# Whole half units of three weight units at the seams of a six-sublayer step, and tiles normalised in another order

## What is computed

```python
def modulate_in(x, g_pre, mod, j):
    return rmsnorm(x, g_pre) * (1.0 + mod[:, :, 3 * j + 1]) + mod[:, :, 3 * j]

def gated_residual(x, out, g_post, mod, j, weight):
    return x + weight * mod[:, :, 3 * j + 2] * rmsnorm(out, g_post)

def shortconv_mixer(h, w_in, conv_w, conv_b, w_out):
    gb, gc, xin = jnp.split(h @ w_in, 3, axis=-1)
    return (gb * dwconv_centred(gc * xin, conv_w, conv_b)) @ w_out

def swiglu(h, w13, w2):
    a, g = jnp.split(h @ w13, 2, axis=-1)
    return (jax.nn.silu(g) * a) @ w2
```

## Time and profile before

| | us |
|---|---|
| median of 3 runs | 2453.85 (2453.64 to 2454.42) |
| profiled execution | 2452.03 |
| its span | 2450.2 |
| PE busy | 2404.4 (98%), granted clock 0.998 |
| DVE busy | 1757.9 (72%) |
| ACT busy | 981.3 (40%) |
| POOL busy | 436.1 (18%) |

### The profile page before, as it was taken

One profiled execution on the slowest core, in us unless ns is written; L12 is line 12 of the kernel. 1 busy time (PEld: TensorE's weight loads), 2 busy tenths in 40 slices (PEclk: granted clock), 3 DMA queues, 4 the chain that ended last, 5 costly groups with the idle time before them and its releaser, 6 DMA issues. The chain is left out here.

```text
span 2450.2 us, 38986 instructions
## 1 busy us (share of the span) xinstructions
PE 2404.4 (98%) x15173; PEld 2204.5 (90%) x15173; DVE 1757.9 (72%) x2469; ACT 981.3 (40%) x1917; POOL 436.1 (18%) x462
## 2 busy tenths in 40 slices
PE   6999999999999999999999999999999999999998
PEld 6998999889889789979988997998899989989997
DVE  5988785675554679778846878885577759856863
ACT  4442343533445455324434442443511154423432
POOL 1220120201115222102213210220200022201211
PEclk9999999999999999999999999999999999999999
DMA  7526333385212453353252426334154433243333
GB/s 228 164 61 217 94 86 128 115 261 154 54 51 74 108 181 87 125 160 87 78 172 104 131 71 229 87 87 138 52 180 139 135 107 90 71 148 98 87 111 113
DMA packets 347229, 297.96 MB, mean 122 GB/s; under 512 B 38799, under 2 KB 296839, under 8 KB 347047
## 3 DMA queue, kind: packets, MB, share of 16 engines
q1 hardware_dynamic: 341798, 278.64, 37.7%
q0 software_dynamic: 5248, 16.83, 1.8%
HBM read 280.57 MB, written 14.80 MB: 121 GB/s over the span
## 5 line engine op out<-in xcount | busy, mean ns | idle before, releaser
L2013 DVE TENSOR_TENSOR w_lo<-w_raw,w_hi 128x512 fp32r<-128x512 f32 (+1 forms) x249 | 211.4, 852 | 243.6 <-ACT w_hi L1419 242.6
L1419 ACT ACTIVATE w_hi<-w_raw 128x512 fp32r<-128x512 f32 (+1 forms) x249 | 188.3, 760 | 467.1 <-DMA w_raw<-in_ffn_w_dram 201.5
L913 PE MATMUL psum<-w_hi,act_hi 128*128 128x512 f32 x800 | 318.3, 398 | 0.4 <-DVE w_lo L2013 0.4
L915 PE MATMUL psum<-w_hi,act_lo 128*128 128x512 f32 x800 | 317.2, 396 | 0.0
L914 PE MATMUL psum<-w_lo,act_hi 128*128 128x512 f32 x800 | 317.0, 396 | 0.0
L1046 PE MATMUL psum<-hT_hi,w_hi 128*128 128x320 f32 x912 | 281.9, 309 | 0.5 <-DVE z_quarters L2301 0.5
L1048 PE MATMUL psum<-hT_hi,w_lo 128*128 128x320 f32 x912 | 281.8, 309 | 0.0
L1047 PE MATMUL psum<-hT_lo,w_hi 128*128 128x320 f32 x912 | 281.8, 309 | 0.0
L1046 PE MATMUL psum<-t_hi,w_hi_more 128*128 128x320 f32 x608 | 187.9, 309 | 0.0
L1048 PE MATMUL psum<-t_hi,w_lo_more 128*128 128x320 f32 x608 | 187.9, 309 | 0.0
L1047 PE MATMUL psum<-t_lo,w_hi_more 128*128 128x320 f32 x608 | 187.8, 309 | 0.0
(11 more groups left out here) (303 smaller groups left out, 5926.4 us busy)
## 6 DMA issues: line engine op xcount, KB each, us to landing
w_raw<-in_ffn_w_dram SPq DMA_DIRECT2D x96, 512.0 KB, 5.1
w_raw_next<-in_ffn_w_dram SPq DMA_DIRECT2D x80, 512.0 KB, 5.2
w_raw<-in_ffn_w_dram SPq DMA_DIRECT2D x148, 256.0 KB, 3.2
ada_tile_ffn<-in_ada_w_dram SPq DMA_DIRECT2D x56, 512.0 KB, 3.9
ada_direct<-in_ada_w_dram POOLq DMA_DIRECT2D x32, 512.0 KB, 5.7
w_raw<-in_ab_w_in_dram SPq DMA_DIRECT2D x28, 512.0 KB, 4.1
w_raw<-in_sc_w_in_dram SPq DMA_DIRECT2D x24, 512.0 KB, 4.7
ada_tile_sc<-in_ada_w_dram SPq DMA_DIRECT2D x24, 512.0 KB, 3.6
```

What stands on the lines that cost most here:

```text
L913: mm(out, a_hi, b_hi, start=first, stop=False)
L915: return mm(out, a_lo, b_hi, start=False, stop=final)
L1419: A(dst, src, ACT.Copy).then_inc(w_hi_ok, 1)
L2013: V.tensor_tensor(d_, a, b.bitcast(F32), ALU.subtract).then_inc(w_lo_ok, 1)
```

## The change

1. The first three units of sublayers 1 to 5 run as whole half units: units 0, 1 and 2 on the first 320 tokens, then the same on the last 320. Unit 2 gets two PSUM banks of its own. Unit 0, the *lead*, gets raw, high and low buffers of its own; it is loaded during the sublayer before (`load_lead`, behind the loads of the gate and the modulation columns) and split in its out phase.
2. In the seams of sublayers 2 and 5 tile three is turned behind unit 0, and the order of DVE and ACT is written anew: a tile is normalised ahead of the wait for the next tile's evacuation. In all seams the slices between which tiles 0 to 2 are turned are others.
3. `STEPS` of "ab" and "sc" are later by a unit or two; `LOADS` stays. In "sc" the split of unit 3 is moved ahead of the convolution.

The core of the diff:

```diff
-STEPS = {"ffn": [2 + j for j in range(16)], "ab": [1, 1, 2, 2, 3, 3, 4, 4, 5, 6, 7, 9, 10, 10, 11, 11], "sc": [2] + [2 + j for j in range(23)]}
+STEPS = {"ffn": [2 + j for j in range(16)], "ab": [2, 2, 3, 3, 4, 4, 5, 5, 6, 7, 8, 9, 10, 10, 11, 11],
+         "sc": [4, 4, 5, 6, 7, 7, 8, 9, 10, 10] + [11 + j for j in range(14)]}
...
+        lead_at = lambda s: arena + 20 * TOK * 4 + HELD[KD] * 4096 if SUBS[s - 1] == "ab" else j0
+        lead_raw = {s: at(f"w_raw_lead{s}", [P, KD, P], lead_at(s)) for s in range(1, len(SUBS))}
+        lead_hi = {s: at(f"w_hi_lead{s}", [P, KD, P], lead_at(s) + 4096, F32R) for s in range(1, len(SUBS))}
+        lead_lo = {s: at(f"w_lo_lead{s}", [P, KD, P], lead_at(s) + 8192, F32R) for s in range(1, len(SUBS))}
...
+            def load_lead(s):
+                l, f = s // 3, s % 3 // 2
+                w, col = {"ffn": (ffn_w13[l, f], FF), "ab": (ab_w_in[0], COL["qa"]), "sc": (sc_w_in[0], D)}[SUBS[s]]
+                dma(lead_raw[s][:], w.rearrange("(p k) n -> p k n", k=KD)[:, :, col:col + P]).then_inc(lead_loaded, 16)
...
-                        for u in range(SC_IN):
+                        for u in range(1, SC_IN):
                             n = nb + u
                             sp.wait_ge(w_lo_ok, n - 1)
...
                         load_gate(s)
                         load_cols(s + 1)
+                        load_lead(s + 1)
...
-            def unit_part(p, h, c0, c1, ready):
+            def unit_part(s, r, h, ready):
+                n = plan[s][0]["nin"] + r
+                out = (THIRD if r == 2 else IN[n % 2])[:, h, 0:HT]
                 for k in range(KD):
                     if k % (KD // 2) == 0:
                         pe.wait_ge(hT_ready, ready[k // (KD // 2)])
-                    hi, lo = w_hi[:, p, k, :], w_lo[:, p, k, :]
+                    hi, lo = (lead_hi[s][:, k, :], lead_lo[s][:, k, :]) if r == 0 else (w_hi[:, n % 2, k, :], w_lo[:, n % 2, k, :])
                     for a, b in ((hi, hT_hi), (hi, hT_lo), (lo, hT_hi)):
-                        last = mm(IN[p][:, h, c0 - h * HT:c1 - h * HT], a, b[:, k, c0:c1],
+                        last = mm(out, a, b[:, k, h * HT:(h + 1) * HT],
                                   start=(k == 0 and a is hi and b is hT_hi), stop=(k == KD - 1 and a is lo))
                 return last
 
...
-                h0, h3, h4 = [HM(s, 2)] * 2, [HM(s, 3)] * 2, [HM(s, NT - 1), HM(s, NT)]
-                for r, h, c0, c1, ready in ((0, 0, 0, HT, h0), (1, 0, 0, HT, h0),
-                                            (0, 1, HT, 4 * P, h3), (0, 1, 4 * P, TOK, h4), (1, 1, HT, TOK, h4)):
-                    n = ph["nin"] + r
-                    if s and r == 0 and c0 == HT:
-                        turn_x(s, NT - 1)
-                    pe.wait_ge(w_lo_ok, n + 1)
-                    need(pe, in_evac[n % 2], inv(ph, n) - 1)
-                    last = unit_part(n % 2, h, c0, c1, ready)
-                    if c1 == TOK:
-                        last.then_inc(pe_unit, 1)
+                for h in range(2):
+                    for r in range(3):
+                        n = ph["nin"] + r
+                        if h == 0 and r == 1 and not early(s):
+                            turn_x(s, 3)
+                        if h == 0 and r == 2:
+                            turn_x(s, NT - 1)
+                            pe.wait_ge(hmod_ok, HM(s, 3))
+                        pe.wait_ge(*((w_lo_ok, n + 1) if r else (lead_lo_ok, LEAD_LO(s))))
+                        if r < 2:
+                            need(pe, in_evac[n % 2], inv(ph, n) - 1)
+                        last = unit_part(s, r, h, [HM(s, NT - 1), HM(s, NT)] if h else [HM(s, 2)] * 2)
+                        if h:
+                            last.then_inc(pe_unit, 1)
...
+                    if s > 1:
+                        pe.wait_ge(in_evac[UB[s] % 2], inv(plan[s][0], UB[s]) + 1)
...
+                SEAM_TURN = {True: {2: 4, 3: 2, 4: 0}, False: {2: 4, 3: 2, 4: 2}}
                 for t in range(NT):
-                    order = list(range(K)) if t < NT - 1 else ring[0::2] + ring[1::2] + list(range(held))
+                    order = list(range(K)) if t < NT - 1 else ring[1::2] + ring[0::2] + list(range(held))
...
-                        if t >= 2 and s + 1 < len(SUBS) and z == (4 if not early(s + 1) else 3 if t == 2 else 0):
+                        if t >= 2 and s + 1 < len(SUBS) and z == SEAM_TURN[early(s + 1)][t]:
...
+            def split_lead(s):
+                act.wait_ge(lead_loaded, 16 * s)
+                A(lead_hi[s][:], lead_raw[s][:], ACT.Copy).then_inc(lead_hi_ok, 1)
...
+                    if final and u == K and s + 1 < len(SUBS):
+                        split_lead(s + 1)
...
+                finish_tile(s - 1, 0)
+                add_out(s - 1, 0)
+                finish_tile(s - 1, 1)
+                norm_x(s, 0)
+                add_out(s - 1, 1)
+                norm_x(s, 1)
+                finish_tile(s - 1, 2)
+                add_out(s - 1, 2)
+                split_h(s, 0)
+                norm_x(s, 2)
+                finish_tile(s - 1, 3)
+                split_h(s, 1)
+                add_out(s - 1, 3)
+                split_h(s, 2)
+                norm_x(s, 3)
+                finish_tile(s - 1, 4)
+                split(n + 1)
+                add_out(s - 1, 4)
+                split(n + 2)
+                norm_x(s, 4)
+                split_h(s, 3)
+                split_h(s, 4)
 
...
-                        split(n + 2, i, 6)
+                        if not (first(i) and jj == 0):
+                            split(n + 2, i, 6)
...
+                        if first(i) and jj == 0:
+                            split(n + 3)
                         modulate_at(ph, u + 2)
...
-                        split(n + 3, i, 6, shape="out" if last and jj == 1 else None)
+                        if not (first(i) and jj == 0):
+                            split(n + 3, i, 6, shape="out" if last and jj == 1 else None)
                         modulate_at(ph, u + 3)
```

More of the change, by code:

```diff
@@ L97 @@
 UB = [sum(units_of(q) for q in range(s)) for s in range(len(SUBS) + 1)]
+LOADED = lambda n: 16 * (n // 2 + 1 - sum(1 for b in UB[1:len(SUBS)] if b <= n and b % 2 == n % 2))
 class Steps:
@@ L219, in build @@
         act_lo = at("act_lo", [P, HF, TOK], arena + HF * TOK * 4, F32R)
[L220 to L223, removed]
+        upad = at("u_pad", [P, TOK + 3], arena + KD * TOK * 4 + MODC * 4)
+        yconv = at("y_conv", [P, TOK + 1], arena + (HF + KD) * TOK * 4 + MODC * 4)
+        assert MODC + TOK + 3 <= (HF - KD) * TOK
         h_mod = at("h_mod", [P, KD, TOK], where["hT_lo"])
@@ L357, in build @@
         DIRECT_BANK = {0: 7, 1: 5, 2: 7, 3: 7}
+        THIRD = pair(6)
+        THIRD_V = THIRD[:, :, 0:HT]
         OUT = [[4, 5, 6, 7, 0], [1, 2, 3, 4, 5]]
@@ L706, in load_pairs @@
                         sp.wait_ge(w_lo_ok, ph["nout"])
+                    if s and not RAW_SLOT[g] and g - ph["g0"] < 2 and not ph["half"]:
+                        sp.wait_ge(pe_unit, ph["nin"] + 1)
                     if g == ph["g0"] and ph["half"] and plan[s][0]["mods"]:
@@ L1276, in turn_rows @@
                     last.then_inc(col_done, 1)
-                for u in range(2, NU):
+                for u in range(3, NU):
                     n = nb + u
@@ L1377, in _ @@
             for s, kind in enumerate(SUBS):
-                if s:
+                if s and early(s):
                     turn_x(s, 3)
@@ L1383, in _ @@
                         for i in range(1, ph["plain"]):
-                            for r in range(2):
+                            for r in range(1 if s and i == 1 else 0, 2):
                                 in_unit(ph, r, i, 2)
@@ L1391, in _ @@
                     elif kind == "sc":
-                        for r in range(2, 6):
+                        for r in range(3, 6):
                             in_unit(ph, r, 0, 6)
@@ L1494, in boundary @@
                 n = plan[s][0]["nin"]
-                for q in range(NT):
-                    square_out(s - 1, 1, q)
-                    if early(s):
+                if early(s):
+                    for q in range(NT):
+                        square_out(s - 1, 1, q)
                         if q in (1, 2):
@@ L1501, in boundary @@
                             modulate(s, 2, range(KD // 2))
-                            split(n, shape="first")
+                            split(n + 1, shape="first")
                         if q == NT - 1:
@@ L1601, in mixed_in @@
                         prod_split(ph, g0, 0)
-                    if i + 1 < ph["plain"]:
+                    if i + 1 < ph["plain"] and (i or not s):
                         split(nb + 2 + 2 * i)
@@ L1649, in body @@
                         fin = last and r == 5
-                        if not (first(i) and r == 0):
+                        if not (first(i) and r < 2):
                             split(nb + r + 1, i, 6, shape="out" if fin else None)
```

(19 more changed lines are left out.)

92 lines of the change are left out of this document (55 added, 37 removed).

## The result

The changed kernel takes 2458.14 us (median of 20 runs, 2454.99 to 2464.12); the kernel before, run beside it, 2454.79 (20 runs). The ratio is 1.0017 (95% interval 1.0010 to 1.0023): about 4 us slower, where 2 us faster were forecast; the time lies within the range. The profiled execution took 2458.77 with a span of 2457.0; that of before, at 2452.03, was one of its quicker ones, so the two traces differ by 6.7, more than the medians (3.4).

The account below looks back on a forecast made before the run. PE, busy 98% of the span at full clock, was taken as the bound. 19.7 - 9.0 - 8.7 = 2.0 us gained gave 2450.0 against the profiled execution; with the median 1.8 above that, 2451.9, range 2441 to 2461.

Parts of the forecast that it names:

- the steps in the short convolution: Short convolution: later steps hold `ada_w` loads and raw loads behind them, PE stops at units 5 to 8; 8.7 us lost.
- the stop at unit 3 goes: Short convolution: PE's existing stop of 1.6 and 0.16 us at unit 3 was to vanish.
- half units, seams and leads: At sublayers 1 to 5: 19.7 us gained by half units and fewer seam stops, 9.0 lost by lead units.
- The narrow parts: Five seams: matmuls of 192 and 128 columns cost 0.112 us a start each; whole halves save 9.4 (3.0 at least).
- rival D: Seams: narrow matmuls cost in proportion to columns, so whole halves save nothing; 2461.3 us, chance .03.
- Idle time at the five seams: Seams: PE's idle time falls by 5.0 us behind the mixers (sublayers 2, 5) and 3.0 at sublayers 1, 3, 4.
- the leads: Out phases before sublayers 1 to 5: lead loads and splits delay other work; 9.0 us lost (1.2 to 17.5).
- B: Out phases: each lead costs 3.5 us, making the kernel slower, 2460.4 us; chance .19.
- C: Out phases: the leads are covered except in "ab", 3.0 us lost there; 2445.9 us, chance .10.
- Rival A: Short convolution: it doesn't stop, as raw loads have unseen slack; 2441.4 us, chance .18.
- E: Short convolution: raw loads land in 3.6 us as `ada_w` loads do; 2448.3 us, chance .06.
- At nothing: Moved steps in "ab", new waits and reordered work cost nothing; without cover in "ab", up to 4 us.

Follow-up runs that it names:

- e1: The changed kernel with the short convolution's `ada_w` loads from the fourth on issued two units later; 2444.26 us, ratio 0.9957 to the kernel before.
- e2: The kernel before with only the new `STEPS` of "sc"; 2465.37 us, ratio 1.0039.
- e4: As e1, with the first three `ada_w` loads of "sc" also two units later, behind the raw loads of units 3 and 4; 2438.77 us, ratio 0.9934.
- e3: The changed kernel with 18 extra matmuls of 320 columns ahead of units 3, 6 and 8 of "sc"; 2456.81 us, ratio 1.0011.
- e8: The kernel before with the new `STEPS` of "sc" and the `LOADS` of e4, nothing else; 2452.34 us, ratio 0.9987.
- e5: On top of e4, the lead of sublayer 2 loaded behind the ring loads of "ab" and split after their splits; 2440.07 us, ratio 0.9947.

## Why the prediction was wrong, point by point

**Failed: the steps in the short convolution, "Lost: 8.7 (5 to 11)".** The mechanism was right: stops at units 5 to 8, raw loads right behind `ada_w` loads, e1 and e2 take and give them. The size was not. e1 gives back 13.9 and e4 another 5.5, so the stretch loses 19 where the working had 10.4. The trace says the same: the working has unit 9 start 15.8 + 10.5 + 9.6 + 9.6 + 7.05 = 52.6 behind the end of unit 2, and it started 61.7 behind. The 9.1 are made of three things:
- The larger error is the sentence that the stop at unit 3 goes, 5.2 us. In the working unit 3's raw load was there in time. In the list it stands with unit 4's behind the wait for the last modulated tile and three `ada_w` loads, as it did before the change, where unit 3 was needed at 1788.6. The half units want it at 1782.6; it went out at 1775.4, landed 8 us later and stopped PE for 3.08 instead of 0. It also held DVE for the 4.16 shown above, and with it the first two steps and the loads behind them: unit 5 starts at 1803.54, 21.0 behind the end of unit 2 and not 15.8. Taken alone (e1 against e4) this load costs 5.5.
- The rounds from one low part to the next are 11.0, 10.2 and 10.9 us, not 10.5, 9.6 and 9.6: 2.3. The landing was taken at 4.5; the DMA view of the changed kernel (1770 to 1850; answer to the earlier trace rows) has

```profile
ada_tile_sc<-in_ada_w_dram SPq DMA_DIRECT2D x12, 512.0 KB, 3.7
w_raw<-in_sc_w_in_dram SPq DMA_DIRECT2D x9, 512.0 KB, 5.0
```

  The estimate of 3.2 from the Trainium skill's fit ("DMA: Bandwidth & Descriptors", "Anatomy of one DMA"; made for GpSimd's path) is further off still.
- The low clock was in no term. Behind unit 8's stop it adds 1.6: unit 9 starts 8.7 after unit 8 and not 7.05. Behind the others it fills time in which PE would have waited, so the stops at 5 to 8 show only 9.35 of idle time; e3 shows that the two can't simply be added.

**Held in sum: half units, seams and leads.** 19.7 - 9.0 = 10.7 was forecast, e8 to e4 is 13 (9 to 17). The narrow parts are gone. Rows of the kernel before that the prediction did not have give the parts of 128 columns 0.112 a start (21 steps), as it assumed, so rival D falls:

```profile
494.63 0.27 PE L940 MATMUL psum<-hT_lo,w_hi 128*128 128x128 f32 x1
...
496.98 0.27 PE L940 MATMUL psum<-hT_lo,w_hi 128*128 128x128 f32 x1
```

No run takes the narrow parts back alone. The rule that the prediction set against this term ("TensorE: Matmul & The Clock Gate", "Back-to-back issue gap" in the Trainium skill) is there the gap of an isolated matmul, and the section says that it under-counts at small N in a stream of weight loads and matmuls; it was no witness against the term.

Idle time at the five seams without the stops at unit 3 fell from 11.3 to 5.2, by 6.1 where 8.0 was said: behind the mixers 5.0 as forecast, behind the FFNs 1.1 and not 3.0. One thing the new seams save was not priced: e2 and e8, whose seams are those of the kernel before, have the low clock behind tile three's stop at sublayer 2 (granted 0.57 from 872 to 876, by an estimate from that some 1.7 us), which the profiled execution of the kernel before lacks.

**Not priced apart: the leads.** In "ab" the stops rose from 0.61 to 2.94, by 2.3 where 3.0 was said for the whole lead. But a low clock follows them, and the 840 to 848 windows, granted 0.50 and 0.73, make that some 3 us more, an estimate: above the upper bound of 3.5. e5 shows that the cost is not in the place of the load alone: there ACT and DVE have the lead's two splits to do ahead of the first turn. In the out phase of "sc" PE waits 0.7 in all. What the three leads in the out phases of FFNs cost, no run shows. B, with 3.5 at each lead, falls, since it leaves 19.7 - 17.5 = 2.2 where 13 was measured; its 2460 is near the result by chance. C (covered but for "ab") stays open: its 19.7 - 3.0 = 16.7 lies between 9 and 17 as the forecast's 10.7 does.

**Rival A** (no stops) falls by the trace; **E** (3.6) by the landing. **"At nothing"** held: no stop in "ab".

So a step that was right in kind carried the sum. It came out 9 us too dear, the rest some 3 better than forecast (e4, without stops, is 16 below the kernel before, where 12.5 was worked out for that case), and a small gain became a small loss. That the time lies within the range owes something to these errors of opposite sign.

## What to carry to other kernels

When an engine's work moves earlier, list every load that it now needs earlier and read each one's issue time and what stands ahead of it in the queue, those the change doesn't touch too. When a step moves later, look for loads that wait for it and then for what stands behind these in the same queue: here one table needed the other moved with it, and that was worth 19 us. A move that pays at its own place can be tested apart by giving the old kernel the same tables (e8).

## What the runs showed of the hardware that was not expected

Three stops of PE of over 3 us in "sc" (3.08, 3.66, 3.61) were each followed by 3.4 to 5.9 us of matmuls at twice the pitch, those of 0.74 and 1.34 by none; two stops of 1.11 and 1.83 close together in "ab" were followed by some 6 us at granted 0.50. Shorter ones had it too: 2.15 in e3 and 2.86 in e2. And the same stop need not give the same clock: the pair of 1.62 and 0.79 at sublayer 2 was followed by a low clock in e8 (0.57 from 872 to 876), but not in the profiled execution of the kernel before (1.00):

```profile
872.00:876.00 4.00, 4.00 (x18) 4.00 (x18) 2.92 (x4) 3.12 (x8) 0.83 (x3) 0.57 0.02 4
```

Filling a stop with other matmuls kept the clock at that place (e3, unit 3), but where a chain on other engines sets the next start, the time saved came back as waiting, and the low clock with it.
